# A two-layer hybrid trunk on one core: the first panel between the w_ada pieces, mLSTM gates stacked on partitions, one attention step reordered

## The reference, cut to what matters

```python
mod_l = silu(c) @ w_ada[layer] + b_ada[layer]          # six parts: shift, scale, gate, twice
p_l = split_columns(modulate(rms_norm(x, norm1), sh1, sc1) @ w_in[layer])   # same for ctx
hm_l, hm_c = mlstm_bidirectional(...)   # 4 heads, 2 directions, gates i and f per token
ya_l = latent_attention(rope(rms_norm(q)), keys(ctx + latent), values)      # 8 heads
yc_l = conv_branch(...)
x = x + g1 * merge_branches(ym_l, ya_l, yc_l, ...)
x = x + g2 * squared_relu_mlp(modulate(rms_norm(x, norm2), sh2, sc2), w_up, w_down)
# layer 0 does the same for ctx; layer 1 needs only its keys, values and states
```

## Time and profile before

| | us |
|---|---|
| median of 3 runs | 1872.4 (1869.42 to 1876.41) |
| the profiled execution | 1873.39 |
| its span | 1871.7 |
| PE busy | 1838.4 (98%) |
| DVE, ACT, POOL busy | 1047.0, 690.6, 159.6 |

### The profile page before, as it was taken

How to read it: one execution, slowest core, us unless ns; L and a number is a source line. 1 busy time by engine, 2 the same in 40 slices (tenths; PEclk the granted TensorE clock), 3 DMA queues, 4 the chain that set the end, 5 groups by cost and what they waited for, 6 DMA issues and landing times.

```text
span 1871.7 us, 24652 instructions
## 1 busy us (share of the span) xinstructions
PE 1838.4 (98%) x10085; PEld 1554.3 (83%) x10085; DVE 1047.0 (56%) x1538; ACT 690.6 (37%) x951; POOL 159.6 (9%) x160
## 2 busy tenths in 40 slices
PE   7999999999999999999999999999999999999998
PEld 4787788888888888878888888788997899999997
DVE  4435643545456675467665655654646656566555
ACT  3423543333222222243232223433544444445444
POOL 2101100001110001320000000300100110120000
PEclk8999999999999999999999999999999999999999
DMA  9221122212444444626444535232242365574563
GB/s 326 71 88 46 46 90 68 68 46 68 135 135 135 135 152 141 205 88 202 135 135 135 176 117 181 68 113 71 65 136 90 93 223 181 187 241 158 187 195 113
DMA packets 214271, 245.51 MB, mean 131 GB/s; under 512 B 5820, under 2 KB 186384, under 8 KB 214160
## 3 DMA queue, kind: packets, MB, share of 16 engines
q1 hardware_dynamic: 213856, 243.85, 40.3%
q10 hardware_dynamic: 304, 0.10, 0.0%
HBM read 242.88 MB, written 1.05 MB: 130 GB/s over the span
## 4 chain that ended last, share of the span: by engine, by line
PE 92%; DVE 3%; ACT 1%; issue 1%; POOL 0%; DVEq 0%; ACTq 0%; POOLq 0%
PE pp L1133 19%; PE pp L1137 19%; PE pp L1134 19%; PE pp L1142 4%; PE pp L1140 4%; PE pp L1141 4%; PE pc L1330 3%; PE pp L1078 2%; PE pp L1079 2%; PE pp L1080 2%; PE pc L1382 2%; PE pc L1039 2%; PE pc L1037 2%; PE pc L1038 2%; PE pc L1420 1%; PE pc L1397 1%
## 5 line engine op out<-in xcount | busy, mean ns | idle before, releaser
L1858 DVE TENSOR_TENSOR wL<-raw,wH 128x1024 fp32r<-128x1024 f32 x358 | 451.2, 1301 | 235.0 <-ACT wH L1434 232.1
L1133 PE MATMUL pp<-hH,wH 128*128 128x512 f32 (+1 forms) x1712 | 574.1, 346 | 2.4 <-ACT hH L1644 2.4
L1134 PE MATMUL pp<-hH,wL 128*128 128x512 f32 (+1 forms) x1712 | 562.9, 339 | 0.0
L1434 ACT ACTIVATE wH<-raw 128x1024 fp32r<-128x1024 f32 x360 | 360.3, 1049 | 299.8 <-PE pp L1142 106.9
L1137 PE MATMUL pp<-hL,wH 128*128 128x512 f32 (+1 forms) x1712 | 441.3, 339 | 1.1 <-POOL hL L1831 0.6
L1133 PEld LDWEIGHTS pp<-hH,wH 128*128 128x128 f32 x1712 | 325.2, 190 | 46.7 <-issue 12.2
L1134 PEld LDWEIGHTS pp<-hH,wL 128*128 128x128 f32 x1712 | 325.2, 190 | 36.7 <-issue 2.2
L1137 PEld LDWEIGHTS pp<-hL,wH 128*128 128x128 f32 x1712 | 295.5, 190 | 37.8 <-POOL hL L1796 1.4
L1133 PE MATMUL pp<-yH,wH 128*128 128x512 f32 (+1 forms) x320 | 115.7, 368 | 0.0
L1140 PE MATMUL pp<-yH,wH 128*128 128x512 f32 (+1 forms) x320 | 114.3, 357 | 0.0
L1142 PE MATMUL pp<-yH,wL 128*128 128x512 f32 (+1 forms) x320 | 114.3, 357 | 0.0
(11 more groups left out here) (270 smaller groups left out, 2250.7 us busy)
## 6 DMA issues: line engine op xcount, KB each, us to landing
raw<-in_w_in SPq DMA_DIRECT2D x84, 1024.0 KB, 5.3
raw<-in_w_up SPq DMA_DIRECT2D x32, 1024.0 KB, 5.5
raw<-in_w_down SPq DMA_DIRECT2D x32, 1024.0 KB, 5.2
pair_W<-in_w_ada SPq DMA_DIRECT2D x10, 2048.0 KB, 8.0
ada_Y<-in_w_ada SPq DMA_DIRECT2D x10, 1024.0 KB, 12.4
ada_H<-in_w_ada SPq DMA_DIRECT2D x8, 1024.0 KB, 11.0
raw<-in_w_proj_m SPq DMA_DIRECT2D x8, 1024.0 KB, 5.1
raw<-in_w_proj_a SPq DMA_DIRECT2D x8, 1024.0 KB, 5.2
```

Source lines behind the costliest of these rows:

```text
L1133: pe.matmul(dsts[b], wh[b], hi[:, kt, ts_], start=first, stop=False)
L1134: pe.matmul(dsts[b], wl[b], hi[:, kt, ts_], start=False, stop=False)
L1434: act.activation(wH[:, p % HIGH, a:a + KH, :], raw[:, p % RAW, a:a + KH, :], ACT.Copy).then_inc(wH_ready, 1)
L1858: dve.tensor_tensor(wL[:, p % RAW, ks, :], raw[:, p % RAW, ks, :], wH[:, p % HIGH, ks, :].bitcast(F32), ALU.subtract).then_inc(wL_ready, 1)
```

## The change: what it does

1. Head: DVE copies all of `xT` (eight copies), from four banks in turn; ACT loads the square root's table before the squares. SP loads w_ada pieces 2 and 3 ahead of the second panel. DVE's `adarow` of quarter 0 stands ahead of `normed`. The first panel's first two K tiles are taken with wH first and wL after ("late"), mk 1 starts after quarter 1, each of quarters 0 and 1 has one `warm` matmul. POOL makes wL of the first two K tiles alone; DVE makes the others.
2. Gates: the token rows and their reversed copy stand on partitions 0 to 63 and 64 to 127 of one tile `g_both`, so one matmul with a wider `sel` gives i on rows 0 to 7 and f on rows 32 to 39. The four row tensors stand at partitions 0, 32, 64, 96 of one tile `four_rows` (zeroed by POOL), so four matmuls of 32 columns give the columns.
3. Layer 1: `weigh` and `weigh_late` of head 0 stand ahead of the last mv panel, in banks 1, 2, 3.
4. Attention, both layers: in rounds 0 and 1 `qss` stands ahead of `probs`. In `qrot` DVE reads both halves out of the bank first, and multiplies by the cosine after.

```diff
@@ make_plan, layer 0
+            step("adarow", l, g=0)
             step("normed", l, j=0)
-            for j in range(NC):
-                step("adarow", l, g=j)
...
+            step("adaturn", l, g=0)
+            step("modulation", l, g=0)
+            step("warm", l, n=1)
+            step("first_high", l, p=0)
+            step("apply", l, n=1, j=0)
+            step("first_low", l, p=0)
+            part("mk", l, 0, 0, 0, 2)
+            plan[-1]["late"] = True
+            step("normed", l, j=1)
+            ada(2)
+            step("adarow", l, g=1)
+            step("adaturn", l, g=1)
+            step("modulation", l, g=1)
+            step("warm", l, n=1)
+            step("apply", l, n=1, j=1)
+            part("mk", l, 0, 0, 2, 4)
+            step("first_high", l, p=1)
+            step("first_low", l, p=1)
+            part("mk", l, 1, 0, 0, 2)
+            step("normed", l, j=2)
+            ada(2)
+            step("adarow", l, g=2)
+            part("mk", l, 1, 0, 2, 3)
+            step("adaturn", l, g=2)
+            step("modulation", l, g=2)
+            step("apply", l, n=1, j=2)
+            part("mk", l, 1, 0, 3, 4)
+            step("normed", l, j=3)
+            part("mk", l, 0, 0, 4, 5)
+            ada(2)
+            step("adarow", l, g=3)
+            part("mk", l, 0, 0, 5, 6)
...
+            step("apply", l, n=1, j=3)
+            part("mk", l, 1, 0, 4, 6)
@@ make_plan, mLSTM and attention
         step("gate_cols", l)
+        if not more:
+            step("weigh", l, h=0)
+            step("weigh_late", l, h=0)
         panel("mv", l, 3)
...
+            if i < 2:
+                step("qss", l, j=3 + i)
             if 1 <= i <= AH:
                 step("probs", l, h=i - 1)
-            if i < 2:
-                step("qss", l, j=3 + i)
@@ banks
-                use(st, kt, (0, 3)[kt % 2])
+                use(st, kt, (0, 3, 1, 2)[kt])
...
-                use(st, name, i % 4)
+                use(st, name, i + 1 if st["h"] == 0 and not whole else i % 4)
@@ SP
             load_panel(0)
+            for a in range(2, 4):
+                load_ada(a)
             load_panel(1)
@@ PE, run_panel
+                if "late" in st:
+                    pe.wait_ge(wH_ready, 2 * p + 1)
+                    for kt in range(KT)[kts]:
+                        for now, of in ((high_of[ready], hi), (ready, lo)):
+                            pe.wait_ge(now, need(kt))
+                            for b in range(NB):
+                                pe.matmul(..., wH[:, hs_, kt, b * P:(b + 1) * P], of[:, kt, ts_], ...)
+                    pe.wait_ge(wL0_ready, 1)
+                    for kt in range(KT)[kts]:
+                        for b in range(NB):
+                            pe.matmul(..., wL[:, ls_, kt, b * P:(b + 1) * P], hi[:, kt, ts_], ...)
+                    return
@@ PE, gates
-                    for name, g in (("i", 0), ("f", 1)):
-                        b = claim(u[name])
-                        pe.matmul(b[0:8, :], sel[0:48, 2 * g, :], rows["g_rows"][:, :], start=True, stop=False)
-                        last = pe.matmul(b[0:8, :], sel[0:48, 2 * g + 1, :], rows["g_back"][:, :], start=False, stop=True)
-                        filled(last, u[name])
+                    b = claim(u["if"])
+                    filled(pe.matmul(b[0:40, :], sel, g_both[:, :], start=True, stop=True), u["if"])
...
-                    for i, name in enumerate(("a_run", "a_back", "e_run", "e_back")):
-                        for tt in range(TT):
-                            c0 = (i * TT + tt) * 8
-                            last = pe.matmul(b[:, c0:c0 + 8], rows[name][0:8, tt * P:(tt + 1) * P], ident[0:8, 0:8],
-                                             start=True, stop=True)
+                    firsts = ident.rearrange("p (i n) -> p i n", i=4)[:, :, 0:8]
+                    for tt in range(TT):
+                        last = pe.matmul(b[:, tt * 32:(tt + 1) * 32], four[:, tt * P:(tt + 1) * P], firsts,
+                                         start=True, stop=True)
@@ ACT
+                    act.wait_ge(s_const, 4)
+                    act.activation(small[:, 13:14], eps, ACT.Sqrt)
@@ POOL
+                        pool.memset(four[:, :], 0.0).then_inc(four_zeroed, 1)
@@ DVE
-                    for kp in range(1, KT // 2, 2):
+                    for kp in range(KT // 2):
...
+                    for b_ in range(NB):
                         start_link(dve.tensor_tensor(dst[b_], dst[b_], ropeC, ALU.mult))
```

More of the change, by code:

```diff
@@ L79, in make_constants @@
     ang = (pos[d // 64][:, :] * inv[d % 32][:, None]).astype(np.float32)
-    sel = np.zeros((P, 4, 8), np.float32)
+    sel = np.zeros((P, 40), np.float32)
     for g in range(2):
@@ L294, in make_plan @@
+            ada(2)
+            step("adarow", l, g=3)
+            part("mk", l, 0, 0, 5, 6)
+            step("adaturn", l, g=3)
+            step("modulation", l, g=3)
+            step("apply", l, n=1, j=3)
+            part("mk", l, 1, 0, 4, 6)
             step("first_rest", l)
@@ L573, in trunk @@
         yL = at("yL", [P, KT, TOK], F32R, o); o += K16
[L575 to L578, removed]
+        names = ["f_pre", "f_neg", "f_exp", "log_f", "F_run"]
+        rows = {n: at(n, [16, TOK], F32, Y + (2 + i) * TOK * 4) for i, n in enumerate(names)}
+        g_both = at("g_both", [P, TOK], F32, Y)
+        four = at("four_rows", [P, TOK], F32, Y + TOK * 4)
         rows["ones"] = at("ones_row", [16, TOK], F32, Y + 11 * TOK * 4)
@@ L964, in _ @@
             load_panel(0)
+            for a in range(2, 4):
+                load_ada(a)
             load_panel(1)
-            for a in range(2, 2 * NC):
+            for a in range(4, 2 * NC):
                 load_ada(a)
@@ L1121, in run_panel @@
                 seen = 0
+                if "late" in st:
[4 more added lines that the diff above has]
+                            for b in range(NB):
+                                pe.matmul(pp[:, slot, b, ts_], wH[:, hs_, kt, b * P:(b + 1) * P], of[:, kt, ts_],
+                                          start=kt == 0 and of is hi, stop=False)
+                    pe.wait_ge(wL0_ready, 1)
+                    for kt in range(KT)[kts]:
+                        for b in range(NB):
+                            pe.matmul(pp[:, slot, b, ts_], wL[:, ls_, kt, b * P:(b + 1) * P], hi[:, kt, ts_],
+                                      start=False, stop=False)
+                    return
                 for kt in range(KT)[kts]:
@@ L1169, in _ @@
                 elif k == "warm":
-                    for i in range(WARM):
+                    for i in range(st["n"]):
                         pe.matmul(pp[:, 1, 1, :], ident, x_in[:, 0, 0:TOK], start=True, stop=True)
@@ L1462, in _ @@
                     half = st["half"]
-                    for kp in range(0, KT // 2, 2):
-                        b = bank(act, u[kp])
-                        act.activation(xT[:, 2 * kp:2 * kp + 2, half * LAT:(half + 1) * LAT],
-                                       b.rearrange("p (j t) -> p j t", j=2), ACT.Copy).then_inc(free[u[kp][0]], 1)
                     for tt in (2 * half, 2 * half + 1):
@@ L1661, in _ @@
                         act.activation(M_parts[i][0:8, :], rows[n][0:8, :], ACT.Copy).then_inc(MH_ready, 1)
-                    act.activation(rows["e_run"][0:8, :], rows["e_run"][0:8, :], ACT.Exp).then_inc(eexp_ready, 1)
+                    act.activation(four[64:72, :], four[64:72, :], ACT.Exp).then_inc(eexp_ready, 1)
                 elif k == "weigh":
@@ L1786, in _ @@
                         pool.memset(wg[:, :, :].bitcast(F32), 0.0).then_inc(wgz_ready, 1)
-                    if st["n"] == 1 and l == 0:
-                        first_rest(j)
+                    if st["n"] == 1 and l == 0 and j == 0:
+                        first_rest()
                     for kt in (2 * j, 2 * j + 1):
@@ L1888, in _ @@
                     dve.reciprocal(n_rs[:, :], n_sd[:, :]).then_inc(x_rs_ready, 1)
-                elif k == "first_split" and st["p"]:
+                elif k == "first_low":
                     split(PANELS[st["p"]])
@@ L2156, in _ @@
                     dve.wait_ge(s_wg, 80 * (l + 1))
-                    b = bank(dve, u["f"])
-                    freed(dve.tensor_scalar(R["f_pre"], b[0:8, :], gb[0:8, 1:2], None, ALU.add), u["f"])
-                    dve.wait_ge(free[u["f"][0]], u["f"][1] + 1)
+                    b = bank(dve, u["if"])
+                    link(dve.tensor_scalar(R["f_pre"], b[32:40, :], gb[32:40, 1:2], None, ALU.add))
                     dve.scalar_tensor_tensor(out=R["f_neg"], in0=R["f_pre"], scalar=-1.0, in1=R["f_pre"],
```

104 lines of the change are left out of this document (40 added, 64 removed).

## The result

| | before | changed |
|---|---|---|
| median, us | 1873.3 | 1851.7 (1850.1 to 1854.0) |
| ratio, 95% interval | | 0.9886 (0.9863 to 0.9909) |
| the profiled execution; its span | 1873.39; 1871.7 | 1850.26; 1848.5 |

Both medians are of four runs. The change makes the kernel 21.6 us faster (17 to 26 by the interval); 1853 was predicted. The prediction's sum held to 1.8 us, but three of its terms were off, the gates' too small, those of the head and of round 1 in layer 1 too large. Most of these errors come from what PE's granted clock does.

The account below looks back on a forecast made before the run. PE bounds the kernel, busy 1838.4 of 1871.7 us. Terms 10.5 + 4.75 + 1.1 + 4.1 - 1.0 + 0.35 = 19.8 us gave 1853.6 from the profiled 1873.4, 1852.6 from the median; 1853 was said, range 1846 to 1862.

Parts of the forecast that it names:

- Gates, 10.5: Both layers: one selection matmul instead of four, four turning matmuls instead of sixteen, 5.25 us less per layer, 10.5 in all.
- Head, 4.75: Start of the kernel: `gate_tok` starts at 57.55 instead of 62.30, 4.75 us gained, range 1.5 to 6.
- a rival's mechanism: Head: clock low in quarter 1 too, 2 to 3 us less gain, 1856; chance 0.17 together with the round 1 fall.
- `value` of head 0, 1.1: Layer 1: PE's wait of 1.1 us for POOL's mask goes, 1.1 us gained; nothing if another wait stands close behind.
- Round 1 of layer 1, 4.1: Attention: new wait of 1.3 us replaces 2.5, 1.2 gained, plus 2.9 from the clock held; 4.1 us together.
- 0.15 for a fall: Rival: the clock falls in layer 1's attention round 1 all the same, only 16.9 us gained, 1856.5; chance 0.15.
- the rule that the prediction weighed: Transposes don't count as PE activity for the clock in the same way; by it round 1 gains 1.2, sum 16.9.
- Layer 0's scores, -1.0: Layer 0, attention round 1: DVE's copies wait for the root of `qss`, scores start 1.0 us later; bounds 0 and -2.
- Rotary, 0.35: Rotary product: bank free one DVE instruction of 0.33 us earlier, of a wait of 0.6; 0.35 us gained.

Follow-up runs that it names:

- gates_only: The kernel before with the gates' edits alone; median 1858.2 us, ratio 0.9925 to before.
- cols16x32: The changed kernel with each of the four turning matmuls issued four times over, sixteen of 32 columns; median 1860.7 us, ratio 0.9932 to before.
- cols16x8: The changed kernel with the columns turned by sixteen matmuls of 128 partitions and 8 moving columns each; median 1862.2 us, ratio 0.9940 to before.
- round_early: The changed kernel with ACT rounding the second panel ahead of hH of quarter 1 instead of behind it; median 1854.6 us, ratio 0.9917 to before.
- head_only: The kernel before with the head's edits alone; median 1872.5 us, ratio 0.9995 to before.
- l0_back: The changed kernel with qss behind probs again in layer 0 alone; median 1852.2 us, ratio 0.9891 to before.

## Why the prediction was right, and where its terms were off

- *Gates, 10.5*: the matmuls gave 10.7 (2.55 and 2.8 a layer), the step for both prices was right. The term was still too small: with the clock it is 15.0 (14.0 by the ratio). The prediction read the clock only behind pauses and not behind the turning matmuls, where the trace before already showed 0.61 and 0.57. That is the step that it lacked, shown by `gates_only`, `cols16x32` and `cols16x8`.
- *Head, 4.75*: 3.2 in the first trace, 1.8 to 2.9 in the seven others that leave the head as the change has it. The steps held to quarter 1 (`adaturn` at 30.14, forecast 29.9). Two failed. The second panel's wL was to be ready at 35.2 and was at 37.4: ACT ended its rounding at 35.3 as forecast, but the sum had counted nothing for DVE's subtraction behind it. DVE took 3.01 us for the two halves instead of 2.35 (as in `round_early`), beside POOL's hL:

```profile
32.58 2.60 POOL L1822 TENSOR_TENSOR hL<-n_h,hH 128x512 fp32r<-128x512 f32 x2 [7.31 <-ACT hH L1670]
34.38 3.01 DVE L1885 TENSOR_TENSOR wL<-raw,wH 128x1024 fp32r<-128x1024 f32 x2 [1.61 <-ACT wH L1462]
36.31 0.50 PE L1165 MATMUL pp<-hH,wH 128*128 128x512 f32 x1 [0.22 <-DVE wL L1885]
```

  PE needs only the first half there and waited 0.22. It reached quarter 2's `adaturn` at 42.66 instead of 41.5; the rest of this 1.2 is small, 0.24 at quarter 1's `adaturn` and a few tenths each at hH, at hL and in the 12 matmuls (2.99 instead of 2.7). And the clock was to be low for a short time only, full from 26.6 on: the head lost 1.7 us by it in two traces and 3.4 in the other six. That was a rival's mechanism, in quarter 0 instead of 1. The mean of the eight starts of `gate_tok` is 59.8; against 62.1 for the two traces with the old head, 2.4. The runs of `head_only` can't confirm this (0.8, with 3.2 as one end of the interval).
- *`value` of head 0, 1.1*: the mask ends at 1265.6 and `value` starts at 1275.33 without a wait. Right by the trace; no run has this edit alone.
- *Round 1 of layer 1, 4.1*: the new wait was forecast at 1.3 and is 1.18, in place of 2.50. The sum had the clock as held, 2.9 more, with 0.15 for a fall; 1.7 is the average gain, because it falls behind the longer wait in 3 of 4 traces and behind the shorter in 4 of 8. Here the rule that the prediction weighed, on transposes and the clock (the Trainium skill, "TensorE: Matmul & The Clock Gate", "Part 4: PE-mode transpose"), is left open: the same eight transposes with the same pause were followed by either level.
- *Layer 0's scores, -1.0*: measured -1.0, by `l0_back`. The wait is 0.78.
- *Rotary, 0.35*: the wait went from 0.6 to 0.3. Right.

With these sizes the sum is 15.0 + 2.4 + 1.1 + 3.0 - 1.0 + 0.3 = 20.8; measured was 21.6. That the total came out within 1.8 us is in part luck: the missing 4.5 in the gates cancelled 3.5 too much in the head and in round 1.

Why a given execution's clock falls at one place and not at another is open: no run here tells it.

## What to carry to other kernels

Read the granted clock behind every stretch of very small matmuls, not only behind waits: here four stacked matmuls instead of sixteen saved 2.8 us of matmuls a layer and, on average, about 2 more of clock. Where an edit's gain hangs on the clock, give it as a chance times a price and look at several executions, since one trace showed 3.4, 1.7 or 0 for the same code. A buffer moved out of the way (an earlier `qss`, its own bank) is worth more than a swap that only shortens the wait and makes a new one in the other layer.

## What the runs showed of the hardware that was not expected

- Sixteen float32 matmuls with 8 or 32 moving columns hold PE 0.22 to 0.23 us each, and behind them the granted clock fell to 0.50 to 0.64 in windows of 4 us in 7 of 8 places, without a wait of PE.
- At a place where the clock fell at all, the loss came out near 1.7 or 3.4 us (up to 5.1 in the head), and whether it fell differed between traces of the same instructions. In `cols16x32` the runs' times go with it (1856.3 us at a mean clock of 0.997, 1863.3 at 0.993).
- A POOL subtraction of 128x512 takes 1.28 us alone; two took 4.83 beside DVE's subtraction of SBUF operands, which kept its 1.18 each (`round_early`). In the changed kernel, where DVE began 1.8 us after POOL, POOL kept 2.60 for its two and DVE's two took 3.01.
